# When raw expert weights are released, and where VectorE splits w1's first half

## What is computed

```python
def expert_block(args):
    xb, e = args
    return (jax.nn.silu(xb @ w1_l[e]) * (xb @ w3_l[e])) @ w2_l[e]
```

## Time and profile before

| | us |
|---|---|
| median of 3 runs | 2255.3 (2254.22 to 2261.86) |
| the profiled execution | 2257.2 |
| its span | 2255.6 |
| PE busy in the span | 2078.8 |
| DVE busy | 1473.0 |
| ACT busy | 959.6 |
| POOL busy | 620.8 |

### The profile page before, as it was taken

How to read it: one execution, slowest core, us unless ns; L and a number is a source line. 1 busy time by engine, 2 the same in 40 slices (tenths; PEclk the granted TensorE clock), 3 DMA queues, 4 the chain that set the end, 5 groups by cost and what they waited for, 6 DMA issues and landing times. The chain is left out here.

```text
span 2255.6 us, 36291 instructions
## 1 busy us (share of the span) xinstructions
PE 2078.8 (92%) x11832; PEld 1640.7 (73%) x11833; DVE 1473.0 (65%) x2839; ACT 959.6 (43%) x1547; POOL 620.8 (28%) x612
## 2 busy tenths in 40 slices
PE   6999999999899999994889999898998898899998
PEld 5878888888788888883666666666676676667775
DVE  5888888888566665565877655555567645646554
ACT  4434344444422222322665555545566544523332
POOL 1121110111334333331333313333334323133332
PEclk9999999999999999996999999999999999999999
DMA  6113322343543333323988777666788865643441
GB/s 230 61 65 119 119 87 91 119 160 101 189 108 128 121 121 117 103 90 115 352 296 296 265 260 265 245 242 245 256 308 303 287 218 199 254 166 128 158 141 48
DMA packets 160047, 404.62 MB, mean 179 GB/s; under 512 B 18999, under 2 KB 25711, under 8 KB 159602
## 3 DMA queue, kind: packets, MB, share of 16 engines
q1 hardware_dynamic: 138582, 346.87, 43.5%
q0 software_dynamic: 13504, 37.08, 5.2%
q10 hardware_dynamic: 7908, 20.06, 2.3%
HBM read 333.78 MB, written 88.36 MB: 187 GB/s over the span
## 5 line engine op out<-in xcount | busy, mean ns | idle before, releaser
L2444 DVE TENSOR_TENSOR w_lo<-raw,w_hi 128x2048 fp32r<-128x2048 f32 x163 | 446.3, 2768 | 126.7 <-ACT w_hi L2345 126.7
L2345 ACT ACTIVATE w_hi<-raw 128x2048 fp32r<-128x2048 f32 x194 | 365.7, 1912 | 76.1 <-DMA raw<-in_w 75.8
L249 PE MATMUL bank<-w_hi,mix_x 128*128 128x512 f32 x816 | 332.8, 408 | 10.1 <-DVE w_lo L232 3.8
L251 PE MATMUL bank<-w_hi,mix_x 128*128 128x512 f32 x816 | 323.0, 396 | 0.0
L250 PE MATMUL bank<-w_lo,mix_x 128*128 128x512 f32 x816 | 322.2, 395 | 0.0
L2301 PE MATMUL bank<-w_hi,x_pair 128*128 128x512 f32 x512 | 203.0, 396 | 19.9 <-DVE x_pair L2436 19.9
L2192 POOL TENSOR_TENSOR w_lo<-raw,w_hi 128x2048 fp32r<-128x2048 f32 x31 | 141.8, 4575 | 229.1 <-ACT w_hi L2345 229.0
L2303 PE MATMUL bank<-w_hi,x_pair 128*128 128x512 f32 x512 | 201.7, 394 | 0.0
L2302 PE MATMUL bank<-w_lo,x_pair 128*128 128x512 f32 x512 | 201.5, 394 | 0.0
L249 PEld LDWEIGHTS bank<-w_hi,mix_x 128*128 128x128 f32 x816 | 156.2, 191 | 42.2 <-issue 4.8
L251 PEld LDWEIGHTS bank<-w_hi,mix_x 128*128 128x128 f32 x816 | 155.9, 191 | 34.4
(11 more groups left out here) (376 smaller groups left out, 4056.0 us busy)
## 6 DMA issues: line engine op xcount, KB each, us to landing
raw<-in_w SPq DMA_DIRECT2D x190, 1024.0 KB, 12.4
y_dram<-in_x_prompt SPq DMA_DIRECT2D x12, 1472.0 KB, 6.9
xT_dram<-mix_x SPq DMA_DIRECT2D x34, 512.0 KB, 3.5
mix_x<-xT_dram SPq DMA_DIRECT2D x34, 512.0 KB, 4.5
y_dram<-y_sb ACTq DMA_DIRECT2D x32, 512.0 KB, 8.1
shared<-in_w_in SPq DMA_DIRECT2D x24, 512.0 KB, 7.0
small<-in_x_prompt SPq DMA_DIRECT2D x16, 512.0 KB
xr_h<-in_x_prompt SPq DMA_DIRECT2D x16, 512.0 KB
```

Of the source, the lines that this page charges most:

```text
L249: pe.matmul(bank[:, :], x_hi[:, k, :], wh[:, k, :], start=(k == 0), stop=False)
L251: ins = pe.matmul(bank[:, :], x_lo[:, k, :], wh[:, k, :], start=False, stop=(k == KD - 1))
L2345: return act.activation(out, in_, ACT.Copy)
L2444: dve.tensor_tensor(w_lo[m][:, cols], raw_of(s, m)[:, cols], w_hi[m][:, cols].bitcast(F32), ALU.subtract).then_inc(signal, 1)
```

## The change

SP no longer waits for `tails_done` but for the up products of the last unit, `t_up_mm` at the step's end, and for each half's split, w1's too. PE doesn't wait for w1's splits ahead of the second down half any more. DVE splits w1 c 0 of the next step between `up` and `hid`, in all steps but the last; before, it stood behind `hidT_lo`. No arithmetic is added or removed.

```diff
@@ SP, step
                             if tailed:
-                                sp_.wait_ge(tails_done, s + 1)
+                                end = entry_of(sp_, 1, s + 1, MAXT, 1)
+                                sp_.wait_ge(t_up_mm, end)
+                                sp_.sem_inc(turn, 1)
                             for m in range(2):
                                 for c in range(2):
-                                    if m or not tailed:
-                                        wait_lo(sp_, s + 1, m, c)
+                                    wait_lo(sp_, s + 1, m, c)
@@ PE, step
                             else:
                                 down_first(s)
-                            if tailed:
-                                for c in range(2):
-                                    wait_lo(pe, s + 1, 0, c)
                             for k in range(KF):
@@ DVE, step
                             STT(up[:, :], tanh_h[:, :], 1.0, H1[:, :], ALU.add, ALU.mult).then_inc(up_done, 1)
+                            if not last:
+                                split(s + 1, 0, (0,))
                             dve.wait_ge(up_done, s + 1)
                             dve.wait_ge(h3_mm, s + 1)
...
-                            split(s + 1, 0, (0,))
                             x_halves(s + 1)
                             split(s + 1, 1, (0,))
```

## The result

The changed kernel takes 2148.0 us (median of 4 runs, 2145.4 to 2155.4) against 2255.4 us: a ratio of 0.952, 95% interval 0.949 to 0.955. Its profiled execution took 2146.1 us with a span of 2144.3. Measured again it was 2150.7 against 2257.4 us.

A forecast was written before the change was run, and what follows sets the result against it. PE, busy 92%, was taken as the bound, losing time to late loads and x. Raw waits 58.2, slow clock 34.1 and x wait 17.9 go, 6.5 come: -103.7, so 2152 us; 8 in 10 range 2138 to 2195.

The forecast's parts named there:

- The sum: Whole kernel: 110.2 us go, 6.5 come, so -103.7 against the profiled 2257.2 us; 2152 us as median.
- Raw waits: PE's waits for raw weights before a tail's up products, line 2274: 58.2 us in 17 pieces, all to go.
- Slow clock behind them: Up products of line 2274 run at the lower clock after the long wait: 34.1 us, to go.
- The x wait: PE's wait at line 2301 for DVE's low half of x: 17.9 us in 13 pieces, to go.
- The first step's cost: POOL's split starts first there, so DVE's moved split delays hid: 6.5 us on PE's path, once; bounds 0 to 9.
- The slack of the loads: A plain step's last load lands in 6 to 8 us, 3 to 5 us before PE asks for it.
- rival A: Loads come earlier but not early enough: 2167 us, or 2198 if half of waits and clock stay; chance 0.18.
- That the release's part was 92 us and the split's 18: Raw waits of 58.2 and slow clock of 34.1 us go by earlier loads, x wait of 17.9 by the moved split.
- DVE ahead of POOL: After the first step DVE's moved split takes the shared port first, ending 4.7 us behind the tanh; POOL's ends at 9.3.
- What is late next: ACT's tail tanh comes 1.0 us after the up products; nothing shows, as PE has twelve down products before needing hid.
- Rival B: POOL gets the port first, hid 5.7 us late: 2323 us if in most steps (0.05 with POOL cutting in); few, 0.03.
- Rival C: The release does nothing, only the x wait goes: 2244 us; chance 0.06.

The follow-up runs named there:

- experiment 3: The kernel before, with 13 unused matmuls of 512 columns where PE waits for raw weights ahead of a tailed step's first unit: 2230.4 us, ratio 0.988.
- experiment 7: The changed kernel with DVE's split of w1's first half at its old place in the first step alone: 2150.3 us, against 2150.7 beside it.
- Experiments 1 and 2: Against the kernel before: the earlier release alone (DVE's order as before), 2215.2 us, ratio 0.982; DVE's moved split alone, 2219.9 us, ratio 0.984.
- experiment 4: The changed kernel, with DVE's moved split held until ACT has made both high halves of w1, when POOL may start too: 2176.1 us, ratio 0.964.
- experiment 8: The changed kernel with DVE's old order in the first step, plus the first down half done once, x transposes in its place: 2159.6 us.

## Why the prediction was right, and where it wasn't

**The sum.** Predicted 2152 us, measured 2148. Against the profiled executions: -103.7 us predicted, -111.1 measured. Raw waits: 58.2 predicted, 57.8 gone. Slow clock behind them: 34.1 predicted, 33.8 gone (125.1 to 91.3), and experiment 3 shows the cause by itself. The x wait: 17.9, all gone.

**The missing 7.4 us.** From the first tanh of the loop to the last the time fell from 877.3 to 764.2 us, 113.1, which is 9.4 more than the sum; what lies outside the loop took 2.0 us more. Of the 9.4, 3.7 are the first step: predicted +6.5, it grew from 22.5 to 25.3 in the profiled execution, because DVE was first there. Another 3.9 are slow clock that I hadn't looked for; the rest is spread over the other steps. Two plain steps of before, with x waits of 1.91 and 1.93 us, took 22.6 and 22.5 us from tanh to tanh; less their waits that is 20.7 and 20.6, where all others behind the first one take under 19; the window behind the first of these waits shows the low clock (columns as in rows 6):

```profile
1571.00:1574.00 3.00, 3.00 (x8) 2.31 (x7) 3.00 (x2) 1.41 (x1) 0.00 (x0) 0.50 0.97 343
```

Against the 18.7 us of today, that is 2.0 and 1.9 us. I had summed the slow clock of line 2274 alone.

**The first step's cost** was right as a mechanism (up to 29.9 us when POOL is first, 7.4 more than before) and wrong as a term: experiment 7 shows that it is worth nothing, since the loads hold the third step otherwise. I charged 6.5 us for a delay and credited 4.1 us of wait and 2.6 of slow clock that this delay itself absorbs; the two cancel, so the sum came out by luck at that place.

**The slack of the loads** is the step that failed. The issue times of the last two loads were right to 0.1 us: 12.7 and 14.9 us behind the tanh for 12.6 and 14.8. The landing was not: 6 to 8 us were estimated for the last load, and it takes 10.3. The estimate doesn't even follow from its own terms: two or three halves of 2.6 us and a start of about as much are 7.8 to 10.4 us, which would have left a slack of 0.9 to 3.5. What moved in those 10.3 us was 3.64 MB at 354 GB/s: 2.85 MB of SP's loads, nearly three halves, and 0.79 MB of stores and gathers of other engines, which the estimate didn't count, at less than the 408 GB/s that it assumed. The slack is 0.7 us, not 3 to 5. The reading "late request, then a full queue" was right for before, but I took it that the queue would be nearly empty afterwards; it is nearly full from release to landing (0.98 of the engines' time at 349 GB/s from 1267.3 to 1306.1, 1.01 at 362 GB/s from 1281 on), and the last load comes only just early enough. So the forecast of "no waits" held in part by luck, by a margin much thinner than it claimed, and rival A was closer than it looked. Experiments 1 and 2 show what waits that stay cost: with one half of the change alone the time was 2215 or 2220.

**That the release's part was 92 us and the split's 18** is wrong as an account of who does what. The split gives 65 us on top of the release (2215 to 2150), the release 69 on top of the split.

**DVE ahead of POOL.** Right in all 30 steps behind the first: 4.7 and 9.3 us behind the tanh were predicted for the two ends, 4.7 and 9.2 measured. (In 7 of the 30, those ahead of an expert with more than one unit, POOL's split comes much later and the two don't meet.) In the first step, where POOL was predicted first, it went either way. The rule from the Trainium skill ("SBUF — State Buffer", "Who interferes with whom") was in doubt for want of a row with DVE first; the changed kernel's 4.78 us and experiment 4's 6.68 us of POOL supply it, and they agree: the later one waits to the end of the earlier.

**What is late next** was right too: the tail's tanh comes 1.0 us behind the up products (1311.52, where these end at 1310.49, 1306.83 plus 3.66), and PE shows no wait for it, because of the down half that experiment 8 tried to save.

**Rival B** was priced at 5.7 us a step. Where it happened, in the first step, DVE was held by the mechanism that it names (6.34 us of split in place of 2.29), but no other step came to it, so the price was never put to the test. **Rival C** is out: its time was 2244, and the release takes 69 us off the moved split alone.

**One sign was off.** SP's wait in a tailed step was to become about 6 us shorter; it became 11 us shorter (202.7 us in 17 pieces for 368.0 in 16). The cause wasn't looked for.

## What to carry to other kernels

When a transfer is late, draw the queue from the first request that follows a gap to the landing that is waited for: what counts is when that stretch starts and how many bytes lie in it, not the latency of the last request. Two edits that each shorten it can be worth less alone than together (here 42 and 37 us, together 107), so test a pair with both singles before giving either the credit. And a wait of 3 us on TensorE may cost 6: compare the duration of the work behind the wait with the same work undisturbed, everywhere, not only behind the longest wait.

## What the runs showed of the hardware

A two-input subtraction on VectorE and one on GpSimd that meet run one after the other in either order: GpSimd's 4.50 us became 6.68 when VectorE started 0.07 us before it, VectorE's 2.29 us became 6.34 when GpSimd started 0.31 us before it. VectorE's `hid` products, which have one operand in PSUM, weren't touched: they took 0.75 us at 1286.53 with GpSimd's split running beside them, as they did at 1311.09 without it.

Matmuls whose result nobody reads, put into 3 us of waiting, kept the granted clock at its upper level (1.00 from 1282 to 1297, behind one of them) and shortened the kernel by 27 us. Of the x waits of 1.9 us some were followed by the low clock (0.50 at 1571 to 1574) and of the two raw waits of 1.85 us neither was (3.66 us for the 64 up products behind each, one of them in rows 3); what makes the difference wasn't tried.
